# Selector scores of the second row tile computed as three products of high and low halves

## The chip, the cores and the metric

One core of one Trainium2 chip runs the kernel. The metric is the device time of one execution in microseconds. Below, TensorE is called PE in the profile, VectorE DVE, ScalarE ACT, GpSimd POOL; "L789" is line 789 of the kernel before.

## The reference, cut to what matters

The network is two layers with three kinds of attention, followed by one block of another kind (attention, convolution, feed-forward). All of it is float32, for 256 tokens of width 2048. The part that the change touches is the selector of the sparse attention ("dsa"), in each of the two layers:

```python
rel = jax.nn.relu(jnp.einsum('bqhi,bki->bqhk', qib, k_idx).astype(jnp.float32) * idx_scale)
score = jnp.einsum('bqhk,bqh->bqk', rel, wb.astype(jnp.float32))
...
_, sel = lax.top_k(score, topk)
```

There are 16 selector heads of width 64 and one selector key of width 64 per token; the 64 best keys of each query are kept. The queries are handled in two row tiles of 128 tokens. The first row tile sees 128 keys, the second 256.

## The kernel before, in words

**Weights.** The kernel streams 394 MB of weights in blocks of 128 x 1024 numbers through four buffers. For each block `g`, ACT rounds it (`round_block`, L903, `high<-raw`), DVE or POOL subtracts what was rounded off (`low_part`, L479, `low<-raw,high`; POOL takes the odd blocks 40 to 133 of a layer), and PE multiplies both parts with rounded activations and their rests (`weight_block`, L644 to L680). These products are in float32r, which PE takes in one pass; plain float32 products (attention, the selector scores) take it two instructions each.

**Order of the work.** Each layer has 162 slots `b`, one weight block each. In slot `b`, PE runs `weight_block`, then index scores, then attention work (`attention`: the values of the job from slot `b - 4`, then new scores). ACT first rounds block `b + 3` and then does `layer_side(b)`; DVE the same with `low_block(b + 3)`. So ACT and DVE are up to three blocks ahead of PE with the weights, and work on everything else in an order fixed by the program: whatever waits in `layer_side(b)` holds back the rounding of block `b + 4` and all that follows.

**The slots that matter.** Jobs of the memory attention ("mem", four heads) start in slots 64, 66, 68 and 70. A job runs: scores on PE (L727), maximum on DVE (L1319), exponentials and division on ACT (L935, L946), transposes on PE in the middle of the block of slot `+4` (L741), the copy `pt<-tb` on ACT in the same slot (`prob_copy`, L956), and right behind that block the products with the values on PE (`values`, L760 and L761), which wait for `pt_ready`. The job of slot 64 thus ends in slot 68, that of slot 68 in slot 72, that of slot 70 in slot 74. `y_high` (L966) is the job's last copy on ACT, in slot `+5`.

The selector's queries come from four weight chunks ("iq", m = 0 to 3) that end before slots 70, 74, 78 and 82. There ACT copies a part out (`cross_out`, L923), DVE adds it (`fold`, L1255) and rotates the chunk (`rope`: L1277, four times L1280 and last L1283, `work<-cb,yf`, which signals `rot_ready`). `index_scores` runs in slots 84 to 89, f = 0 to 5: f = 0 and 1 are the first row tile (eight heads, 128 keys), f = 2 to 5 the second (four heads each, 256 keys). Even heads lie on partitions 0 to 63 and write `sbank`, odd heads on 64 to 127 and write `obank`:

```python
for e, bank, full in ((0, sbank, s_full), (1, obank, o_full)):
    half = slice(64 * e, 64 * e + 64)
    for c, h in enumerate(heads[e::2]):
        q = iqT[h // 8][half, h // 2 % 4, s * P:s * P + P]
        ins = pe.matmul(bank[:, c * n:c * n + n], q, ikT[half, 0:n], start=True, stop=True)
    ins.then_inc(full, 1)
```

ACT copies both banks out with a ReLU (L1082) and DVE sums them up (L1488, L1490).

Of the kernel before, what the change touches and what calls it, by code (L numbers as in the profile page):

```python
# [36 lines left out]
ALU = mybir.AluOpType  # L37
# [154 lines left out]
SCORES2 = {58 + 8 * (h // 2) + 2 * (h % 2): ("ali", h) for h in range(H2)}  # L192

IDX_AT, TOPK_AT = 84, 90
CONV_AT, CONV_PER_2_SLOTS = 18, 8
GLU_AT = (18, 26, 42, 50)
MEAN_AT, VAR_AT, SILU_AT = 81, 83, 85
# [26 lines left out]
def build(nc, a, out):  # L224
    by, chunk_at, acc_users = plan(a)
    with ExitStack() as ctx:
        def sb(name, shape, dt=F32):
            return ctx.enter_context(nc.sbuf_tensor(name, shape, dt))
# [13 lines left out]
        yhf, ylf = yf[:, 0], yf[:, 1]  # L242
        yh, yl = yhl[:, 0], yhl[:, 1]
        x = sb("x_nat", [P, ST, D])
        work = sb("work", [P, 12528])
        cb = sb("cb", [P, 4, CW])
        sc = sb("sc", [P, 2, ST, S])
# [12 lines left out]
        def cut(t, at, *dims):  # L260

            n = int(np.prod(dims))
            v = t[:, at:at + n]
            if len(dims) == 2:
                v = v.rearrange("p (a b) -> p a b", a=dims[0])
            if len(dims) == 3:
                v = v.rearrange("p (a b c) -> p a b c", a=dims[0], b=dims[1])
            return v
# [27 lines left out]
        vm = [cut(work, 9216 + 1024 * l, ST, 512) for l in range(DEPTH)]  # L296
        ikT = cut(work, 11264, S)
        ndsa = cut(work, 11520, 512)

        q2T, k2T, v2 = cut(work, 0, H2, S), cut(work, 2048, H2, S), cut(work, 4096, ST, 1024)  # L300
        hT = cut(work, 8192, 8, PAD + S)
# [30 lines left out]
        def vec(name, n):  # L332
# [20 lines left out]
            cum_ready decay_ready rel_ready rel_used hi_ready xt_ready var_ready std_ready nmr_ready  # L353
            norm_ready aff_ready sum_ready sq_ready xres_ready rs_ready rt_ready vg2_ready qk2_ready
            sig_ready vraw_ready hT_ready conv_step low_pool yc_ready csq_ready cn_ready silu_ready ch_ready ct_ready
            relu_ready fsq_ready fin_ready out_done dve_done norm_dve rows_half""".split()
        (ident_landed, tables_landed, rows_landed, rowp_landed, rowf_landed, high_ready,
         low_ready, block_used, s_full, o_full, m_ready, e_ready, r_ready, p_ready, pt_ready, y_ready,
         yhi_ready, yt_ready, kq_ready, v_ready, g_ready, rot_ready, nar_ready, flog_in, flog_e, flog_ln,
# [1 line left out]
         hi_ready, xt_ready, var_ready, std_ready, nmr_ready, norm_ready, aff_ready, sum_ready, sq_ready,  # L361
         xres_ready, rs_ready, rt_ready, vg2_ready, qk2_ready, sig_ready, vraw_ready, hT_ready,
         conv_step, low_pool, yc_ready, csq_ready, cn_ready, silu_ready, ch_ready, ct_ready, relu_ready,
         fsq_ready, fin_ready, out_done, dve_done, norm_dve, rows_half) = (sem(n) for n in names)
        mem_landed, x_landed = ([sem(f"{n}_landed{i}") for i in range(4)] for n in ("mem", "x"))
        raw_landed = [sem(f"raw_landed{i}") for i in range(RING)]
        t_full = [sem(f"t_full{i}") for i in range(2)]
# [117 lines left out]
        def _(pe):  # L485
# [291 lines left out]
            def index_scores(l, f):  # L777
                s, n, heads = index_shape(f)
                if f == 0:

                    pe.wait_ge(ikt_ready, l + 1)
                    pe.wait_ge(rot_ready, turned(("iq", l, 3)))
                s_begin(("idx", l, f))
                o_begin(("idx", l, f))
                for e, bank, full in ((0, sbank, s_full), (1, obank, o_full)):
                    half = slice(64 * e, 64 * e + 64)
                    for c, h in enumerate(heads[e::2]):
                        q = iqT[h // 8][half, h // 2 % 4, s * P:s * P + P]
                        ins = pe.matmul(bank[:, c * n:c * n + n], q, ikT[half, 0:n], start=True, stop=True)  # L789
                    ins.then_inc(full, 1)  # L790

# [105 lines left out]
        def _(act):  # L897
# [152 lines left out]
            for l in range(DEPTH):  # L1050
                g0 = LAYER0 + LAYER_SLOTS * l

                def layer_side(b, l=l, g0=g0):
                    new = ends(g0 + b, "fq", "fk", "mq", "mg", "fg", "dg", "iq", "dq", "dk")
                    if b - 4 in SCORES:
                        prob_copy(l, *SCORES[b - 4])
                    if new:
                        cross_out(new)
                    attention(l, b, SCORES)
                    for name in (ends(g0 + b, "mv", "fv", "dv"), ends(g0 + b - 1, "fq", "fk", "mq", "mg", "fg", "dg")):  # L1060
                        if name:
                            copied_out(name)
                    if b == 10:
                        act.wait_ge(block_used, by[("nar", l)].blocks[-1] + 1)
                        act.activation(y[0:NAR, 1, :], sbank[0:NAR, 0:S], ACT.Copy).then_inc(nar_ready, 1)
                    if b == 11:

                        act.wait_ge(flog_in, l + 1)
                        act.activation(fe, fe, ACT.Exp).then_inc(flog_e, 1)
                        act.wait_ge(flog_e, l + 1)  # L1070
                        act.activation(fl, fe, ACT.Ln, bias=1.0).then_inc(flog_ln, 1)
                    if b == 150:
                        root_ahead()
                    if IDX_AT <= b < IDX_AT + 6:
                        f = b - IDX_AT
                        n = 6 * l + f
                        if n >= 2:

                            act.wait_ge(rel_used, n - 1)
                        for e, bank, full, no in ((0, sbank, s_full, s_no), (1, obank, o_full, o_no)):  # L1080
                            act.wait_ge(full, no[("idx", l, f)] + 1)
                            act.activation(rel[f % 2][e], bank[:, :], ACT.Relu, scale=IDIM ** -0.5).then_inc(rel_ready, 1)  # L1082
# [152 lines left out]
        def _(dve):  # L1235
# [168 lines left out]
            for l in range(DEPTH):  # L1404
# [16 lines left out]
                def layer_side(b, l=l, g0=g0):  # L1421
# [35 lines left out]
                        dve.wait_ge(cum_ready, l + 1)  # L1457
                    if name and name[0] in ("iq", "dq", "dk"):
                        rope(name)
                    if IDX_AT <= b < IDX_AT + 6:  # L1460
                        index_sum(l, b - IDX_AT)
                    if TOPK_AT <= b < TOPK_AT + TOPK // 8:
# [427 lines left out]
```

## Time and profile before

| | |
|---|---|
| three runs | 2184.83, 2185.27, 2188.21 us (median 2185.27) |
| the profiled execution | 2182.5 us, its span 2180.7 us |
| PE busy | 2147.4 us (98% of the span) |
| DVE busy | 1280.2 us (59%) |
| ACT busy | 1106.5 us (51%) |
| POOL busy | 405.3 us (19%) |
| mean granted clock of PE | 0.998 |

A row of a timeline gives the start, the length and the name of an instruction or of several alike that follow each other. On PE, starts are the better measure: matmuls are pipelined, so a row's length holds a tail of 0.27 to 0.4 us in which the next already runs. PE is nearly always busy, so what counts is what makes its stream longer, or stops it.

### The profile page before, as it was taken

What the parts mean: (1) busy time and instruction counts of PE and PEld (TensorE: products, weight loads), DVE (VectorE), ACT (ScalarE), POOL (GpSimd) and SP (SyncE); (2) the same over time, 40 slices, a digit from 0 to 9 for tenths busy, and PEclk for the clock granted to TensorE, in tenths of its full rate; (3) what the DMA queues carried; (4) which work ended last, traced back from release to release, by engine and by line L of the source; (5) the groups of instructions that cost most, each with busy time, mean ns of one, the idle gap of its engine ahead of it and who ended that gap; (6) DMA issues with size and microseconds to landing.
All of it is one profiled execution on the core that took longest, in us unless ns stands there. A gap on an engine that the chain in (4) does not pass through costs nothing.

```text
span 2180.7 us, 29518 instructions
## 1 busy us (share of the span) xinstructions
PE 2147.4 (98%) x11780; PEld 1863.0 (85%) x11780; DVE 1280.2 (59%) x1866; ACT 1106.5 (51%) x1537; POOL 405.3 (19%) x176
## 2 busy tenths in 40 slices
PE   8999999999999999999999999999999999999998
PEld 7888988888888898888887888788888888888886
DVE  5544438765576337856576677666555555555556
ACT  4444554554464555555455455646535534544543
POOL 0000333442000333342006886000000000000000
PEclk9999999999999999999999999999999999999999
DMA  8666555655666555665656655545566656666664
GB/s 278 196 180 184 164 149 160 177 171 174 193 187 186 162 155 155 175 173 174 189 178 183 189 179 155 198 149 181 190 194 190 191 194 191 188 193 192 190 191 140
DMA packets 324375, 394.65 MB, mean 181 GB/s; under 512 B 20320, under 2 KB 252384, under 8 KB 323472
## 3 DMA queue, kind: packets, MB, share of 16 engines
q1 hardware_dynamic: 322592, 383.20, 58.2%
q0 software_dynamic: 1648, 9.58, 1.2%
q8 instruction: 93, 1.52, 0.3%
q14 instruction: 42, 0.34, 0.0%
HBM read 390.63 MB, written 2.10 MB: 180 GB/s over the span
## 4 chain that ended last, share of the span: by engine, by line
PE 96%; DVE 2%; ACT 1%; issue 1%; DMA 0%; SPq 0%; DVEq 0%; ACTq 0%
PE acc L661 34%; PE acc L678 18%; PE acc L680 12%; PE acc L665 12%; PE acc L666 11%; PE acc L663 1%; PE acc L644 1%; PE tb L590 1%; PE obank L763 1%; PE tb L741 1%; PE sbank L731 1%; PE sbank L789 1%; ACT high L903 0%; DVE low L479 0%; ACT pt L1003 0%
## 5 line engine op out<-in xcount | busy, mean ns | idle before, releaser
L903 ACT ACTIVATE high<-raw 128x1024 fp32r<-128x1024 f32 (+1 forms) x729 | 763.1, 1050 | 791.9 <-PE acc L661 205.8
L479 DVE TENSOR_TENSOR low<-raw,high 128x1024 fp32r<-128x1024 f32 (+1 forms) x569 | 703.0, 1237 | 617.6 <-ACT high L903 614.8
L661 PE MATMUL acc<-xhl,high 128*128 128x512 f32 x3200 | 769.1, 392 | 2.9 <-ACT cb L1201 1.7
L661 PEld LDWEIGHTS acc<-xhl,high 128*128 128x128 f32 x3200 | 587.8, 189 | 117.3 <-ACT cb L1201 2.1
L479 POOL TENSOR_TENSOR low<-raw,high 128x1024 fp32r<-128x1024 f32 x160 | 397.7, 2489 | 728.7 <-ACT high L903 728.5
L678 PE MATMUL acc<-xhl,low 128*128 128x256 f32 x3200 | 435.6, 286 | 0.7 <-DVE xhl L1712 0.7
L678 PEld LDWEIGHTS acc<-xhl,low 128*128 128x128 f32 x3200 | 414.3, 191 | 16.4 <-DVE xhl L1712 1.1
L665 PE MATMUL acc<-high,yhl 128*128 128x512 f32 (+1 forms) x1044 | 383.1, 373 | 0.0
L666 PE MATMUL acc<-high,yhl 128*128 128x512 f32 (+1 forms) x1044 | 382.0, 372 | 0.0
L680 PE MATMUL acc<-low,yhl 128*128 128x512 f32 (+1 forms) x1044 | 243.7, 374 | 0.2
L665 PEld LDWEIGHTS acc<-high,yhl 128*128 128x128 f32 x1044 | 196.7, 188 | 34.3
L666 PEld LDWEIGHTS acc<-high,yhl 128*128 128x128 f32 x1044 | 196.7, 188 | 34.1
L680 PEld LDWEIGHTS acc<-low,yhl 128*128 128x128 f32 x1044 | 184.5, 189 | 34.1 <-DVE yhl L1356 1.0
L1255 DVE TENSOR_TENSOR acc<-acc,cross 128x512 f32<-128x512 f32 x104 | 72.1, 693 | 70.3 <-ACT cross L923 70.1
L1615 DVE SCALAR_TENSOR_TENSOR tb<-work,params,tb 128x256 f32<-128x256 f32 x232 | 93.5, 479 | 0.0
L935 ACT ACTIVATE sc<-sc,small 128x128 f32<-128x128 f32 x64 | 28.7, 448 | 99.2 <-DVE small L1331 99.2
L680 PE MATMUL acc<-low,xhl 128*128 128x512 f32 (+1 forms) x320 | 71.1, 355 | 0.0
L665 PE MATMUL acc<-high,xhl 128*128 128x256 f32 (+1 forms) x224 | 69.1, 331 | 0.0
L666 PE MATMUL acc<-high,xhl 128*128 128x256 f32 (+1 forms) x224 | 68.6, 329 | 0.0
L923 ACT ACTIVATE cross<-acc 128x512 f32<-128x512 f32 x104 | 60.4, 581 | 0.0
L680 PEld LDWEIGHTS acc<-low,xhl 128*128 128x128 f32 x320 | 51.8, 189 | 8.6 <-issue 1.3
L665 PEld LDWEIGHTS acc<-high,xhl 128*128 128x128 f32 x224 | 42.6, 190 | 4.8 <-issue 0.7
(214 smaller groups left out, 1355.5 us busy)
## 6 DMA issues: line engine op xcount, KB each, us to landing
raw<-in_w_in SPq DMA_DIRECT2D x336, 512.0 KB, 3.7
raw<-in_w_ff SPq DMA_DIRECT2D x256, 512.0 KB, 4.0
raw<-in_w_out SPq DMA_DIRECT2D x91, 512.0 KB, 4.4
raw<-in_w_mem_kv SPq DMA_DIRECT2D x32, 512.0 KB, 5.1
raw<-in_w_out SPq DMA_DIRECT2D x10, 256.0 KB, 2.7
x_nat<-in_mem SPq DMA_DIRECT2D x4, 512.0 KB, 7.9
x_nat<-in_x POOLq DMA_DIRECT2D x4, 512.0 KB, 6.7
yf<-in_ln_gain POOLq DMA_DIRECT2D x2, 1024.0 KB, 5.1
```

Source lines behind the costliest of these rows:

```text
L479: eng.tensor_tensor(part(low, g), part(raw, g), part(high, g).bitcast(F32), ALU.subtract).then_inc(ready, 1)
L590: ins = pe.transpose(t[:, dt * S + s * P:dt * S + s * P + P], src[:, s, first + dt * P:first + dt * P + P], ident)
L661: ins = pe.matmul(acc[:, 2 * (c.acc % 2) + s, :], wh[:, t, at], vhl, start=first, stop=last)
L665: pe.matmul(outs[s], vh[:, at], wh[:, t, :], start=first, stop=False)
L666: ins = pe.matmul(outs[s], vl[:, at], wh[:, t, :], start=False, stop=last)
L678: ins = pe.matmul(acc[:, 2 * (c.acc % 2) + s, S:2 * S], wl[:, t, at], vh, start=False, stop=last)
L680: ins = pe.matmul(outs[s], vh[:, at], wl[:, t, :], start=False, stop=last)
L903: act.activation(part(high, g), part(raw, g), ACT.Copy).then_inc(high_ready, 1)
L923: act.activation(cross, crosses(c), ACT.Copy).then_inc(cross_ready, 1)
L935: ins = act.activation(sc[:, j % 2, s, 0:n], src, ACT.Exp, bias=nmx[:, r:r + 1], accum_out=rs[:, r:r + 1])
L1255: dve.tensor_tensor(accs(c), accs(c), cross, ALU.add).then_inc(folded, 1)
L1615: ins = dve.scalar_tensor_tensor(out=cv[:, ct, :] if tap == TAPS - 1 else sums_at, in0=src, scalar=w, in1=sums_at, op0=ALU.mult, op1=ALU.add)
```

## The change

For f = 2 to 5 the float32 products are replaced by three float32r products each: rounded query by rounded key, rest of the query by rounded key, rounded query by rest of the key. The products of even and odd heads follow each other in turns. The four halves lie where the first attention's queries and keys lay (`work_r` is a float32r name for the same memory as `work`).

- ACT gets five copies in each layer: the rounded key in slot 66, the rounded queries of chunk m in slots 71, 75, 79 and 83, each at the end of the slot's side work, behind a wait for `rot_ready` of that chunk.
- DVE gets five subtractions in each layer, one slot later each, behind a wait for the ACT copy.
- PE waits for `split_ready` ahead of f = 2 to 5. f = 0 and 1 stay as they were.

```diff
 IDX_AT, TOPK_AT = 84, 90
+SPLIT_AT, IQ_SPLIT = 66, (71, 75, 79, 83)
...
+        iqH, iqL = cut(work_r, 0, IH // 2, P), cut(work_r, 1024, IH // 2, P)
+        ikH, ikL = cut(work_r, 2048, S), cut(work_r, 2304, S)
...
                 s_begin(("idx", l, f))
                 o_begin(("idx", l, f))
+                if s:
+                    pe.wait_ge(split_ready, 5 * l + f)
+                    for c in range(2):
+                        at = heads[0] // 2 + c
+                        for part_no, (q, k) in enumerate(((iqH, ikH), (iqL, ikH), (iqH, ikL))):
+                            for e, bank in enumerate((sbank, obank)):
+                                half = slice(64 * e, 64 * e + 64)
+                                ins = pe.matmul(bank[:, c * n:c * n + n], q[half, at, :], k[half, :], start=part_no == 0,
+                                                stop=part_no == 2)
+                                if c == 1 and part_no == 2:
+                                    ins.then_inc((s_full, o_full)[e], 1)
+                    return
...
+                    if b == SPLIT_AT:
+
+                        act.wait_ge(s_full, s_no[("job", job_no(l, "fox", HF - 1))] + 1)
+                        act.wait_ge(ikt_ready, l + 1)
+                        act.activation(ikH, ikT, ACT.Copy).then_inc(kh_ready, 1)
+                    if b in IQ_SPLIT:
+                        m = IQ_SPLIT.index(b)
+                        act.wait_ge(rot_ready, turned(("iq", l, m)))
+                        act.activation(iqH[:, 2 * m:2 * m + 2, :], iqT[m // 2][:, 2 * (m % 2):2 * (m % 2) + 2, P:S],
+                                       ACT.Copy).then_inc(qh_ready, 1)
...
+                    if b == SPLIT_AT + 1:
+                        dve.wait_ge(kh_ready, l + 1)
+                        dve.tensor_tensor(ikL, ikT, ikH.bitcast(F32), ALU.subtract).then_inc(split_ready, 1)
+                    if b - 1 in IQ_SPLIT:
+                        m = IQ_SPLIT.index(b - 1)
+                        dve.wait_ge(qh_ready, 4 * l + m + 1)
+                        dve.tensor_tensor(iqL[:, 2 * m:2 * m + 2, :], iqT[m // 2][:, 2 * (m % 2):2 * (m % 2) + 2, P:S],
+                                          iqH[:, 2 * m:2 * m + 2, :].bitcast(F32), ALU.subtract).then_inc(split_ready, 1)
```

ACT in slots 71 and 72 of the first layer, with the waits that stand ahead of each instruction. Before:

```order
L903 ACTIVATE high<-raw 128x1024 [waits block_used,raw_landed2]
L966 ACTIVATE yhl<-y 128x256 [waits y_ready]
L903 ACTIVATE high<-raw 128x1024 [waits block_used,raw_landed3]
L956 ACTIVATE pt<-tb 128x512 [waits o_full,t_full0]
L946 ACTIVATE sc<-sc,small 128x256 [waits r_ready]
```

With the change (lines are 19 further down):

```order
L922 ACTIVATE high<-raw 128x1024 [waits block_used,raw_landed2]
L985 ACTIVATE yhl<-y 128x256 [waits y_ready]
L1099 ACTIVATE work_r<-work 128x256 [waits rot_ready]
L922 ACTIVATE high<-raw 128x1024 [waits block_used,raw_landed3]
L975 ACTIVATE pt<-tb 128x512 [waits o_full,t_full0]
L965 ACTIVATE sc<-sc,small 128x256 [waits r_ready]
```

The copy of the rounded query and its wait now stand ahead of the rounding of block 75 and of the copy `pt<-tb` of the job from slot 68.

PE in the second row tile's scores, f = 2 of the first layer. Before (each of these float32 matmuls is two in the trace):

```order
L789 MATMUL sbank<-work 128x256 [waits rel_ready]
L789 MATMUL sbank<-work 128x256
L789 MATMUL obank<-work 128x256 x2
```

With the change:

```order
L799 MATMUL sbank<-work_r 128x256 [waits split_ready,rel_ready]
L799 MATMUL obank<-work_r 128x256
L799 MATMUL sbank<-work_r 128x256
L799 MATMUL obank<-work_r 128x256
L799 MATMUL sbank<-work_r 128x256
L799 MATMUL obank<-work_r 128x256
L799 MATMUL sbank<-work_r 128x256
L799 MATMUL obank<-work_r 128x256
L799 MATMUL sbank<-work_r 128x256
L799 MATMUL obank<-work_r 128x256
L799 MATMUL sbank<-work_r 128x256
L799 MATMUL obank<-work_r 128x256
```

Four products in float32 have become twelve in float32r, in turns between the two banks.

## Rows read from the trace of the kernel before

**Rows 1.** The page: busy times; a costly group: count, busy us, mean ns, idle before.

```profile
PE 2147.4 (98%) x11780; PEld 1863.0 (85%) x11780; DVE 1280.2 (59%) x1866; ACT 1106.5 (51%) x1537; POOL 405.3 (19%) x176
...
L678 PE MATMUL acc<-xhl,low 128*128 128x256 f32 x3200 | 435.6, 286 | 0.7 <-DVE xhl L1712 0.7
```

**Rows 2.** PE's timeline at f = 3, first layer: start us, length us, engine, line, names.

```profile
379.63 0.39 PE L666 MATMUL acc<-high,xhl 128*128 128x512 f32 x1
379.94 0.48 PE L789 MATMUL sbank<-work 64*128 64x256 f32 x1
379.96 0.48 PE L789 MATMUL obank<-work 64*128 64x256 f32 x1
380.26 0.38 PE L789 MATMUL sbank<-work 64*128 64x256 f32 x1
...
380.70 0.38 PE L789 MATMUL sbank<-work 64*128 64x256 f32 x1
...
381.35 0.40 PE L666 MATMUL acc<-high,xhl 128*128 128x512 f32 x1
```

**Rows 3.** The same view at f = 0, end of it: weight loads, then matmuls.

```profile
367.61 0.63 PEld L789 LDWEIGHTS obank<-work 64*128 64x128 f32 x5
...
367.72 0.72 PE L789 MATMUL obank<-work 64*128 64x128 f32 x5
```

**Rows 4.** PE's timeline, a run of float32r matmuls of 256 columns on the whole array.

```profile
599.84 4.00 PE L796 MATMUL sbank<-xhl 128*128 128x256 f32 x32
```

**Rows 5.** ACT's timeline, slots 67 to 76 of the first layer.

```profile
312.19 1.05 ACT L903 ACTIVATE high<-raw 128x1024 fp32r<-128x1024 f32 x1
...
314.60 0.60 ACT L956 ACTIVATE pt<-tb 128x512 f32<-128x512 f32 x1
...
328.65 0.41 ACT L966 ACTIVATE yhl<-y 128x256 fp32r<-128x256 f32 x1
328.95 1.05 ACT L903 ACTIVATE high<-raw 128x1024 fp32r<-128x1024 f32 x1
330.11 0.60 ACT L956 ACTIVATE pt<-tb 128x512 f32<-128x512 f32 x1
...
337.38 0.57 ACT L956 ACTIVATE pt<-tb 128x512 f32<-128x512 f32 x1
...
342.04 1.06 ACT L903 ACTIVATE high<-raw 128x1024 fp32r<-128x1024 f32 x1 [1.97 <-PE acc L661]
```

**Rows 6.** PE's timeline: the values of the jobs from slots 64, 68 and 70.

```profile
315.35 0.62 PE L760 MATMUL obank<-pt,work 128*128 128x256 f32 x2
...
330.86 0.62 PE L760 MATMUL obank<-pt,work 128*128 128x256 f32 x2
...
336.72 1.19 PE L678 MATMUL acc<-xhl,low 128*128 128x256 f32 x8
338.06 0.67 PE L760 MATMUL obank<-pt,work 128*128 128x256 f32 x2
```

**Rows 7.** DVE's timeline: the last step of rope for m = 0 and 1.

```profile
330.19 2.81 DVE L1283 TENSOR_TENSOR work<-cb,yf 128x512 f32<-128x512 f32 x1
...
343.86 2.27 DVE L1283 TENSOR_TENSOR work<-cb,yf 128x512 f32<-128x512 f32 x1
```

**Rows 8.** All instructions of line 1283 in that form: shortest, median, longest in ns.

```profile
L1283 DVE TENSOR_TENSOR work<-cb,yf x16: 692/693/2816, 330.2 to 1004.7; 128x512 f32<-128x512 f32 x16
```

**Rows 9.** POOL's timeline in slot 72.

```profile
330.08 2.37 POOL L479 TENSOR_TENSOR low<-raw,high 128x1024 fp32r<-128x1024 f32 x1 [5.20 <-ACT high L903]
```

**Rows 10.** The second layer, slot 72: ACT's timeline, then PE's.

```profile
832.63 0.60 ACT L956 ACTIVATE pt<-tb 128x512 f32<-128x512 f32 x1
...
833.38 0.62 PE L760 MATMUL obank<-pt,work 128*128 128x256 f32 x2
```

**Rows 11.** The last block: PE's timeline; then the stretch behind it (third number from the end: PE's clock).

```profile
1380.94 0.67 PE L763 MATMUL obank<-pt,work 128*128 128x256 f32 x2 [3.37 <-issue]
...
1381.00:1383.00 2.00, 2.00 (x10) 1.73 (x11) 1.93 (x3) 1.97 (x5) 0.00 (x0) 1.00 0.56 178
```

More of the change, by code:

```diff
@@ L244, in build @@
         x = sb("x_nat", [P, ST, D])
+        with nc.sbuf_tensor("work_r", [P, 12528], F32R) as work_r:
+            pass
         work = sb("work", [P, 12528])
@@ L355, in build @@
             sig_ready vraw_ready hT_ready conv_step low_pool yc_ready csq_ready cn_ready silu_ready ch_ready ct_ready
-            relu_ready fsq_ready fin_ready out_done dve_done norm_dve rows_half""".split()
+            relu_ready fsq_ready fin_ready out_done dve_done norm_dve rows_half kh_ready qh_ready split_ready""".split()
         (ident_landed, tables_landed, rows_landed, rowp_landed, rowf_landed, high_ready,
@@ L363, in build @@
          conv_step, low_pool, yc_ready, csq_ready, cn_ready, silu_ready, ch_ready, ct_ready, relu_ready,
-         fsq_ready, fin_ready, out_done, dve_done, norm_dve, rows_half) = (sem(n) for n in names)
+         fsq_ready, fin_ready, out_done, dve_done, norm_dve, rows_half, kh_ready, qh_ready, split_ready) = (sem(n) for n in names)
         mem_landed, x_landed = ([sem(f"{n}_landed{i}") for i in range(4)] for n in ("mem", "x"))
@@ L787, in index_scores @@
                     for c, h in enumerate(heads[e::2]):
-                        q = iqT[h // 8][half, h // 2 % 4, s * P:s * P + P]
+                        q = iqT[h // 8][half, h // 2 % 4, 0:P]
                         ins = pe.matmul(bank[:, c * n:c * n + n], q, ikT[half, 0:n], start=True, stop=True)
```

## The prediction

> **What bounds the kernel now.** I read the page first. PE is busy for 98% of the span [rows 1], so nothing that another engine gains can shorten the run. The change can act in two ways: by the length of PE's own stream, and by new stops in it. I then read the stretch of the scores on PE's timeline. The reader is to see that even and odd heads already run side by side, though the program issues them one after the other: `obank` starts 0.02 us behind `sbank` [rows 2]. So the change cannot win by pairing the halves. Last I read ACT's timeline ahead of the scores beside that of PE, since ACT works in program order, and looked for what stands behind the new waits. What matters there is `pt<-tb`. PE starts the products with the values 0.11 us after the copy has ended where it waited for it (337.38 + 0.57 = 337.95, start at 338.06) [rows 5, 6].
>
> **The part on PE: the scores.** At f = 3 the last ordinary matmul starts at 379.63; ordinary ones of 512 columns follow each other every 0.23 us, so the next would have been due at 379.86. The second one behind the scores starts at 381.35, which puts the stream back in step at 381.12. The pass costs 1.26 us [rows 2]. It holds four pairs of float32 instructions, (380.70 - 380.26) / 2 = 0.22 us apart, hence 4 x 0.22 = 0.88, and 0.38 us for going to half-height tiles and back, which stays.
>
> With the change there are six pairs. A float32r matmul of 256 columns on the whole array comes every (4.00 - 0.28) / 31 = 0.12 us [rows 4]. I take that for a pair, since pairs are seen to start together [rows 2]: 6 x 0.12 + 0.38 = 1.10 us, a gain of 0.16 us. There are eight such passes (f = 2 to 5, two layers): **-1.3 us**. No row shows float32r on half the rows, so the bounds are: 0.11 us a pair, the pace of the shortest matmuls on one half [rows 3], which gives 1.04 and -1.8 us in all; and the halves in turns, 12 x 0.12 + 0.38 = 1.82, which gives +4.5 us in all.
>
> **The weight loads.** In one half, five loads start (0.63 - 0.19) / 4 = 0.11 us apart (0.19 us is the length of one) and the matmuls (0.72 - 0.27) / 4 = 0.11 us apart [rows 3]. A load thus runs while the matmul before it, in the same half, still streams. The Trainium skill (TensorE: Matmul & The Clock Gate, Part 3, The mechanism) says that a weight load overlaps running matmuls only when its row group is another one, which speaks against this change, as each half gets six loads for four. By that rule the sum below would be 5.3 us higher (second rival); rows 3 contradict it, with pairs in one half at 0.11 us.
>
> **The part on ACT: the key, slot 66.** The new copy is like `y_high`, 0.41 us long, and puts off what follows by 0.30 us (328.65 to 328.95), as copies overlap a little [rows 5]. It stands ahead of the rounding at 312.19, and from there ACT has no gap up to the copy `pt<-tb` at 314.60. That copy ended at 315.20 and will end at 315.50; the values start 0.11 us later at 315.61 instead of 315.35 [rows 5, 6]: **+0.3 us** of PE per layer.
>
> **The part on ACT: the queries of m = 0, slot 71.** This is the main term. ACT reaches the new wait when `y_high` is done, at about 329.0. The chunk's rope then still has its last step before it: it begins at 330.19 [rows 5, 7]. Behind the wait stand the rounding of block 75 (now at 328.95) and `pt<-tb` (now at 330.11). How long the last step takes is the question. It took 2.81 us, but that form has a median of 0.693 us [rows 7, 8]. It was stretched while POOL subtracted block 75 from 330.08 to 332.45 [rows 9], and POOL could only do so because ACT had rounded block 75. With ACT held, POOL has nothing, and the step ends at 330.19 + 0.69 = 330.88. The Trainium skill (SBUF — State Buffer, SBUF: two separate sides) calls the pair of ports that DVE and GpSimd share an exclusive lock, held for a whole instruction, also against DVE operations with two SBUF inputs. By it the step should be short when POOL is idle; the trace agrees, as the 2.81 us step ended 0.55 us after POOL's.
>
> So: copy of the queries 330.92, rounding of block 75 from 331.22, `pt<-tb` 0.95 us later (1.05 less the overlap) from 332.17 to 332.77, values at 332.88. Before they started at 330.86 [rows 6]: **+2.0 us** of PE per layer. The second layer stands the same, with `pt<-tb` at 832.63 and values at 833.38 [rows 10], 0.75 us apart as before (330.11 and 330.86).
>
> **What is given back.** The values of the next job started at 338.06 while PE's matmuls ahead of it, from 336.72, were out of the way at 336.72 + 1.19 - 0.29 + 0.13 = 337.75 [rows 1, 6]. That stop of 0.3 us came from ACT being late, since it stood behind the long rope step. With rope over two us earlier and PE two us later, it goes: **-0.3 us** per layer.
>
> **Edits costed at nothing.** m = 1 holds ACT in slot 75 from about 340.1 until rope ends. That end moves from 346.13 to 343.86 + 0.69 = 344.55, again as POOL is idle [rows 7]. Block 79 is then rounded from about 344.9 instead of 342.04 and POOL has its rest at about 348.4. PE needs it three blocks after 342.04; a block is 8 x 0.23 + 8 x 0.12 = 2.8 us, so at 350.4. The cover is 2 us; without it the same stop as in slot 72 would come. No `pt<-tb` stands behind this wait, nor behind those of m = 2 and 3. Behind the last, in slot 83, stand a rounding and the copies of the scores' first banks, which come later than rope ends. DVE's five subtractions of some 0.4 us find DVE 59% busy [rows 1], waiting for PE's values or ACT's roundings around them; if one meets POOL it is late by up to 2.4 us, inside the three blocks that DVE is ahead. PE's new waits ahead of f = 2 to 5 are for queries split in slots 72 to 84, and it gets to them in slots 86 to 89. SP's loads for blocks 79 and 83 are issued 2 to 3 us later, as they wait for POOL's rests; their cover is again the three blocks by which ACT is ahead.
>
> **The clock.** A stop of 3.37 us for the same reason (`pt<-tb` late) stands in the last block, and the stretch behind it shows a granted clock of 1.00, the 2.4 GHz level [rows 11]. A stop of 2.0 us should cost nothing more.
>
> **Sum.** 2 x (0.3 + 2.0 - 0.3) - 1.3 = **+2.7 us** on the profiled execution's 2182.5: 2185.2 us. That execution lies 2.8 us below the median of the three runs, so for the runs I carry +2.7 over to the median: **2188.0 us**. A measurement of this kernel can tell about 0.2%, or 4.4 us, from no change; +2.7 is less.
>
> **Rivals.**
> - *Rope stays long, slower (chance 0.13).* If the last step of rope takes its 2.81 us with POOL idle too, the values of slot 72 wait 2.1 us longer in each layer: +2.7 + 4.2 = +6.9, 2192.2 us. It decides from a step of about 1.6 us on. For it: two of the long steps are just these chunks'. Against it: the median of 0.693 us, and POOL's end 0.55 us before the step's [rows 8, 9].
> - *The halves lose their overlap, slower (0.15).* If a half must finish a product before it takes its next weights, each product takes 0.11 + 0.12 = 0.23 us, a pass 6 x 0.23 + 0.38 = 1.76, and eight passes +4.0 instead of -1.3: +8.0 in all, 2193.3 us. Halves strictly in turns give +8.5. For it: twelve loads where there were eight, in turns. Against it: rows 2 and 3. The Trainium skill's rule named above would be this case.
> - *No stop at all (0.12).* If PE were held at slot 72 by nothing new, because rope and the rounding came earlier than I place them, only the gain in the scores is left: -1.3, 2184.0 us. For it: ACT has gaps on both sides of slot 72. Against it: between wait and values only 0.11 us of slack is seen.
> - *The change does nothing for the scores (inside my forecast).* At 0.147 us a pair a pass costs the same as before and the sum is +4.0.
>
> **How the numbers follow.** The forecast has 0.55, with a range of its own from +0.8 to +4.8; 0.05 is left for longer stops, such as POOL and DVE meeting on a path that matters. The range reaches from the third rival with the scatter of the runs, 2183.5, to the second with the same, 2194. Slower by over 0.2%: the first two rivals, the 0.05, and the upper edge of the forecast, 0.35. Faster by over 0.2% has no mechanism but scatter, 0.03. Within 0.2%: 0.62.
>
> **What would show it.** In the new profile: a pass of the scores of about 1.1 us, six pairs 0.12 us apart; ACT's new copy in slot 71 behind a wait of about 2 us for DVE's rope; L1283's steps of iq all at 0.69 us; PE idle for about 2 us ahead of the values of slot 72, once in each layer, and not ahead of those of slot 74; PE's clock at 1.00 after it. I am wrong if pairs are 0.2 us apart, if PE stops in slots 75 to 89, or if it does not stop in slot 72.

## Result, and the profile after

The changed kernel took **2191.56 us** (median of 12 runs, 2187.25 to 2193.95), beside 2184.94 us for the kernel before (12 runs, 2183.10 to 2188.21). The ratio is **1.0027, 95% interval 1.0018 to 1.0035**: 5.9 us slower, with an interval of 3.9 to 7.6. The forecast was 2.7 us slower and 2188.0 us. The time lies inside the range given, but above the forecast's own +0.8 to +4.8, and past the 0.2% that I had taken as the border of "no change".

The profiled execution took 2191.48 us (span 2189.4) beside 2182.5 (span 2180.7). That is 9.0 us, more than the 5.9 us of the medians; what the rest is, the part on the last block shows. The page hardly shows the difference, since PE is busy at 98% in both; the line answers to [rows 1]:

```profile
PE 2151.1 (98%) x11812; PEld 1867.5 (85%) x11812; DVE 1278.7 (58%) x1876; ACT 1109.6 (51%) x1547; POOL 406.1 (19%) x176
```

The list of what PE waited for does. Here `L767` is the line that was 760, the values `pt` times V, and it had no entry before; `L770` is the old 763, unchanged:

```profile
PE obank L767 <- issue: 3.7, 2, 1.8
PE obank L770 <- issue: 3.4, 1, 3.4
```

Two stops of 1.84 us. PE's timeline around the first, to be laid beside [rows 6]:

```profile
314.58 0.67 PE L767 MATMUL obank<-pt,work 128*128 128x256 f32 x2
...
329.11 1.19 PE L685 MATMUL acc<-xhl,low 128*128 128x256 f32 x8
332.14 0.67 PE L767 MATMUL obank<-pt,work 128*128 128x256 f32 x2 [1.84 <-issue]
...
332.89 2.00 PE L685 MATMUL acc<-xhl,low 128*128 128x256 f32 x8
334.68 4.73 PE L668 MATMUL acc<-xhl,high 128*128 128x512 f32 x16
...
339.61 1.19 PE L685 MATMUL acc<-xhl,low 128*128 128x256 f32 x8
340.64 0.62 PE L767 MATMUL obank<-pt,work 128*128 128x256 f32 x2
```

How to read it: subtract the start of the same instruction before. The values were at 315.35, 330.86 and 338.06; they are at 314.58, 332.14 and 340.64. The lag goes from -0.77 to +1.28 to +2.58 us. The first step, 2.05 us, is the stop. The second, 1.30 us, has no stop in it. It is 1.61 us lost less 0.31 us given back at the values of slot 74. The loss shows in the matmuls: eight of `L685` take 2.00 us where they take 1.30 us in the same place before. The table by stretches says why (the length stands ahead of the comma, PE's busy time behind it, and PE's clock is the third number from the end):

```profile
330.00:332.10 2.10, 0.30 (x3) 0.09 (x1) 1.78 (x4) 1.91 (x4) 0.47 (x1) 1.00 0.00 0
332.10:334.00 1.90, 1.86 (x9) 1.79 (x10) 0.72 (x2) 1.90 (x4) 1.90 (x1) 0.79 0.74 189
334.00:336.00 2.00, 2.00 (x9) 1.71 (x8) 1.80 (x3) 0.15 (x1) 0.04 (x1) 0.50 0.59 139
336.00:338.00 2.00, 2.00 (x9) 1.65 (x8) 0.00 (x0) 0.33 (x1) 0.00 (x0) 0.85 0.94 262
```

Behind the stop the granted clock is 0.50, the 1.2 GHz level, and PE is busy all the same. The second layer is a copy of the first, `L685` at 2.27 us:

```profile
837.66 0.67 PE L767 MATMUL obank<-pt,work 128*128 128x256 f32 x2 [1.84 <-issue]
...
838.47 2.27 PE L685 MATMUL acc<-xhl,low 128*128 128x256 f32 x8
```

The cause of the stop itself, on ACT and DVE in slots 71 and 72, answers to [rows 5, 7]:

```profile
330.19 0.42 ACT L1099 ACTIVATE work_r<-work 128x256 fp32r<-128x256 f32 x1 [1.86 <-DVE work L1312]
330.51 1.04 ACT L922 ACTIVATE high<-raw 128x1024 fp32r<-128x1024 f32 x1
331.46 0.58 ACT L975 ACTIVATE pt<-tb 128x512 f32<-128x512 f32 x1
```

```profile
329.46 0.69 DVE L1312 TENSOR_TENSOR work<-cb,yf 128x512 f32<-128x512 f32 x1
```

ACT is held 1.86 us for rope, then rounds block 75, and only then copies `pt<-tb`, which ends at 332.04; the values start at 332.14. Rope's last step took 0.69 us, where it had taken 2.81. All sixteen in that form now lie between 692 and 695 ns, for a largest of 2816 before [rows 8]. POOL is idle meanwhile, as its next row shows:

```profile
331.63 2.41 POOL L486 TENSOR_TENSOR low<-raw,high 128x1024 fp32r<-128x1024 f32 x1 [7.48 <-ACT high L922]
```

The Trainium skill (SBUF — State Buffer, SBUF: two separate sides) has DVE and GpSimd exclude each other on a shared pair of ports. By that page the step should be short with POOL idle, and the trace agrees.

The scores of the second row tile at f = 3, first layer, beside [rows 2]:

```profile
382.04 0.39 PE L673 MATMUL acc<-high,xhl 128*128 128x512 f32 x1
382.36 0.38 PE L799 MATMUL sbank<-work_r 64*128 64x256 f32 x1
382.36 0.38 PE L799 MATMUL obank<-work_r 64*128 64x256 f32 x1
382.58 0.28 PE L799 MATMUL sbank<-work_r 64*128 64x256 f32 x1
...
382.70 0.28 PE L799 MATMUL sbank<-work_r 64*128 64x256 f32 x1
...
383.05 0.27 PE L799 MATMUL sbank<-work_r 64*128 64x256 f32 x1
...
383.60 0.40 PE L673 MATMUL acc<-high,xhl 128*128 128x512 f32 x1
```

Both halves run together, in pairs (383.05 - 382.58) / 4 = 0.12 us apart, and the pass costs (383.60 - 0.23) - (382.04 + 0.23) = 1.10 us, where it cost 1.26. The weight loads of one half follow each other as closely, each while a matmul of its own half streams (PE's loads at f = 2, then its matmuls):

```profile
378.70 0.18 PEld L799 LDWEIGHTS sbank<-work_r 64*128 64x128 f32 x1
...
378.81 0.19 PEld L799 LDWEIGHTS sbank<-work_r 64*128 64x128 f32 x1
```

```profile
378.69 0.28 PE L799 MATMUL sbank<-work_r 64*128 64x256 f32 x1
...
378.81 0.28 PE L799 MATMUL sbank<-work_r 64*128 64x256 f32 x1
```

### The profile page after: what moved, and what is told of

Same layout as the page of the kernel before. It is cut to its first block, busy times and chain, and to the rows that moved or that the text cites. A ratio compares the mean times of both kernels' runs of the same rounds, so it can differ in the third digit from the quotient of the medians.

```text
span 2189.4 us, 29604 instructions
## 1 busy us (share of the span) xinstructions
PE 2151.1 (98%) x11812; PEld 1867.5 (85%) x11812; DVE 1278.7 (58%) x1876; ACT 1109.6 (51%) x1547; POOL 406.1 (19%) x176
## 3 DMA queue, kind: packets, MB, share of 16 engines
q8 instruction: 94, 1.54, 0.3%
## 4 chain that ended last, share of the span: by engine, by line
PE 96%; DVE 1%; ACT 1%; issue 1%; DMA 1%; SPq 0%; DVEq 0%; ACTq 0%
PE acc L668 35%; PE acc L685 18%; PE acc L687 12%; PE acc L672 11%; PE acc L673 11%; PE acc L670 1%; PE acc L651 1%; PE tb L597 1%; PE obank L770 1%; PE tb L748 1%; PE sbank L738 1%; ACT high L922 0%; ACT pt L1022 0%; PE sbank L737 0%; PE obank L771 0%
## 5 line engine op out<-in xcount | busy, mean ns | idle before, releaser
L685 PE MATMUL acc<-xhl,low 128*128 128x256 f32 x3200 | 437.6, 287 | 0.7 <-DVE xhl L1749 0.7
L685 PEld LDWEIGHTS acc<-xhl,low 128*128 128x128 f32 x3200 | 416.3, 192 | 16.6 <-DVE xhl L1749 1.1
```

Source lines behind the costliest of these rows:

```text
L685: ins = pe.matmul(acc[:, 2 * (c.acc % 2) + s, S:2 * S], wl[:, t, at], vh, start=False, stop=last)
```

## The experiments

Profiled executions start up to 1.4 us apart, and runs of one kernel scatter by some 3 to 4 us to either side, so I use one measure beside the ratio: **the stretch** from the start of the first `sbank<-work` pair of 128 columns past 279 us to that of the first past 950 us. It takes in the scores of both layers and the slots ahead of them, all that the change touches. In the profile of before the two rows are (the second behind the last scores):

```profile
282.73 0.39 PE L730 MATMUL sbank<-work 128*128 128x128 f32 x2
...
955.71 0.39 PE L730 MATMUL sbank<-work 128*128 128x128 f32 x2
```

In the profile after they stand at line 737:

```profile
281.75 0.39 PE L737 MATMUL sbank<-work 128*128 128x128 f32 x2
...
960.73 0.39 PE L737 MATMUL sbank<-work 128*128 128x128 f32 x2
```

So 672.98 before and 678.98 after, +6.00. A second number, **values to values**, is the time from the values of slot 72 to those of slot 74 (332.14 and 340.64 above: 8.50); a slow clock shows in it, a stop ahead of slot 72 does not.

| kernel | stretch, against before | stop ahead of slot 72, per layer | values to values, first layer | ratio of the runs (95%), runs |
|---|---|---|---|---|
| after | +6.00 | 1.84 idle | 8.50 | 1.0027 (1.0018 to 1.0035), 12 |
| after_again | +6.09 | 1.84 idle | 8.54 | 1.0028 (1.0016 to 1.0040), 6 |
| e1_m0_later | +3.19 | none | 7.53, with a stop of 0.47 | 1.0026 (1.0016 to 1.0037), 9 |
| e2_all_later | -0.46 | none | 7.52, with a stop of 0.47 | 1.0011 (1.0002 to 1.0021), 11 |
| e3_wait_only | +2.76 | 1.54 idle | 6.94 | 1.0015 (1.0006 to 1.0024), 11 |
| e4_scores_f32 | +3.88 | 1.84 idle | 6.93 | 1.0026 (1.0017 to 1.0035), 11 |
| e5_stop_filled | +2.90 | filled | 6.94 | 1.0017 (1.0008 to 1.0026), 11 |
| e6_halves_apart | +1.55 | none | 7.20 | 1.0031 (1.0019 to 1.0042), 6 |
| e7_split_late | -0.99 | none | 7.21 | 1.0008 (0.9997 to 1.0018), 11 |
| e7b_split_late_again | -0.99 | none | 7.21 | 1.0001 (0.9991 to 1.0011), 12 |
| e8_split_late_f32 | +0.05 | none | 7.21 | 1.0009 (1.0000 to 1.0017), 11 |
| e10_split_late_shifted | +0.04 | none | 7.23 | 1.0000 (0.9992 to 1.0009), 12 |
| c0_before_again | +0.05 | none | 7.20 | 0.9992 (0.9983 to 1.0000), 11 |

A ratio of 1.001 is 2.2 us. Two kernels that are the same give the same stretch within 0.1 us, while their ratios lie up to 0.0008 from each other or from 1. The 7.20 us of before and of c0, and the 7.20 to 7.23 of e6, e7, e8 and e10, hold the 0.3 us stop of slot 74 [rows 6]; 6.94 is the distance without it.

My theory was the prediction's: ACT held in slot 71 makes `pt<-tb` late, and a later slot for the copy frees it. The rival: ACT is then held elsewhere, and the stop is handed on.

**The wait alone.** The kernel before, with nothing but the new wait on ACT; no copy, no subtraction, no new scores.

```diff
+                    if b == 71:
+                        act.wait_ge(rot_ready, turned(("iq", l, 0)))
```

> The kernel before plus one bare wait: ACT waits for the rotation of m = 0 at the end of slot 71, and does nothing there. Nothing else of the change is in it. Theory 1: PE stops ahead of the values of slot 72 for 0.3 us less than in the changed kernel (no copy behind the wait), 1.7 us, rope's last step is 0.69 us long, 0.3 us comes back in slot 74, and behind each stop PE's clock falls to 1.2 GHz for some us (1.7 us each): 2184.9 + 2 x (1.7 - 0.3 + 1.7) = 2191.1 us, or 2187.7 if a stop of 1.7 us leaves the clock up. Theory 2: within 1 us of before.

```profile
332.78 0.67 PE L760 MATMUL obank<-pt,work 128*128 128x256 f32 x2 [1.54 <-issue]
...
334.67 3.83 PE L661 MATMUL acc<-xhl,high 128*128 128x512 f32 x16
...
339.72 0.62 PE L760 MATMUL obank<-pt,work 128*128 128x256 f32 x2
```

The wait alone makes the stop; the copy itself adds the 0.30 us to 1.84. Per layer: +1.69 of stop, -0.31 given back, 2.76 in all. So the stop comes from what the wait holds back on ACT, not from any work that was added. The clock stayed up behind it here (`L661` x16 at 3.83 us), which the expectation held possible; the median of the runs, 2189.44 us, lies between its two figures, 2191.1 and 2187.7.

**The scores undone, the copies kept.** As after, but the second tile's scores are the float32 products again; the split halves are made and not used.

```diff
                 if s:
                     pe.wait_ge(split_ready, 5 * l + f)
-                    for c in range(2):
...
-                    return
...
-                        q = iqT[h // 8][half, h // 2 % 4, 0:P]
+                        q = iqT[h // 8][half, h // 2 % 4, s * P:s * P + P]
```

> The changed kernel with its copies, subtractions and waits, but the second row tile's scores in plain float32 as before. Theory 1: slower than the changed kernel by what the new products gain, 1.3 us: 2192.9 us, ratio to before 1.0036. Theory 2 (the new products save nothing, or lose): the same time as the changed kernel or less.

The stops are the same 1.84 us in both layers, but the clock did not fall behind either of them in this profiled execution: values to values 6.93 and 6.94 us, where after has 8.50 and 8.53. The stretch is +3.88. Against e5's +2.90, which has the same slots and a full clock too, the scores are worth 0.98 us; e7 against e8 gives 1.04. The forecast was 1.3. The ratios (1.0026 beside after's 1.0027) read as the expectation's second theory, that the new products save nothing. They can't show that, since after's profile has the two spells of slow clock and e4's has not, and a microsecond is less than their scatter.

**The stop filled.** As after, with 16 matmuls whose result nobody reads in the place of the stop. They begin once the last exponent of the job has left `sbank`.

```diff
+                if table is SCORES and b == 72:
+                    pe.wait_ge(e_ready, job_no(l, "mem", 3) + 1)
+                    for _ in range(16):
+                        pe.matmul(sbank[:, 0:S], xh[:, 0, 0:P], xh[:, 0, :], start=True, stop=True)
```

> The changed kernel with 16 matmuls more in slot 72 of each layer, ahead of the products with the values: float32r, 256 columns, on data that is at hand, into a bank that nobody reads. Theory 1 (PE stops for 2 us, and because it stood still its clock falls behind the stop): the values still start when pt<-tb is done, 2.0 us late, but PE is busy until then, and the clock stays at 2.4 GHz in both layers. The profile of the changed kernel lost 1.6 us a layer there, so up to 3.2 us less than the changed kernel's 2191.6: 2188.4 us. Theory 2 (the low clock there is chance and costs little on average): the same as the changed kernel within 1 us.

```profile
331.24 2.08 PE L778 MATMUL sbank<-xhl 128*128 128x256 f32 x16
333.25 0.67 PE L767 MATMUL obank<-pt,work 128*128 128x256 f32 x2
...
335.14 3.83 PE L668 MATMUL acc<-xhl,high 128*128 128x512 f32 x16
```

```profile
333.00:335.00 2.00, 2.00 (x14) 1.79 (x13) 0.61 (x2) 2.00 (x5) 2.00 (x1) 1.00 0.62 167
```

The values are as late as in after, 3.04 us behind the `L685` group of 330.21 (after: 332.14 - 329.11 = 3.03), and nothing was saved in waiting. Yet the stretch is 3.1 us shorter than after's, because the clock stays at 1.00. This separates the two parts of the loss: 2.9 us of lateness and other terms, 3.1 us of clock. The runs agree in direction (1.0017 beside 1.0027, median 2188.52 us for the 2188.4 expected), but the intervals overlap.

**The copies moved.** Same work, other slots. The row of numbers is (key, m = 0 to 3).

```diff
-SPLIT_AT, IQ_SPLIT = 66, (71, 75, 79, 83)
+SPLIT_AT, IQ_SPLIT = 66, (72, 75, 79, 83)
```

> The changed kernel with one number changed: the copy of the rounded queries of m = 0 stands in slot 72, behind the copy pt<-tb, not in slot 71. Theory 1 (the cost is the stop ahead of the values of slot 72, and the lower clock behind it): that stop goes in both layers, so does the half-speed stretch; left are the scores' gain of 1.3 us and 0.3 us a layer from the key's copy in slot 66. Expected 2184.9 - 1.3 + 0.6 = 2184.2 us, ratio to before 0.9997 +- 0.0008. Theory 2 (the waits of m = 1 to 3 or the added work on ACT and DVE cost it): at most the 2 x 2.0 us seen as idle go, the ratio stays at 1.001 or above.

This missed. The stop of slot 72 is gone, as theory had it, but the stretch is still +3.19. 0.3 us comes back at slot 74, and 1.5 us per layer in slots 75 to 84. ACT and POOL of that stretch (the time in brackets is idle time before, and what ended it):

```profile
345.96 0.42 ACT L1099 ACTIVATE work_r<-work 128x256 fp32r<-128x256 f32 x1 [4.52 <-DVE work L1312]
...
347.40 4.96 POOL L486 TENSOR_TENSOR low<-raw,high 128x1024 fp32r<-128x1024 f32 x2 [7.03 <-ACT high L922]
```

DVE beside them, and two of the places where PE then stops:

```profile
347.44 2.66 DVE L1495 TENSOR_TENSOR work_r<-work,work_r 128x256 fp32r<-128x256 f32 x1
350.02 3.43 DVE L486 TENSOR_TENSOR low<-raw,high 128x1024 fp32r<-128x1024 f32 x1
```

```profile
362.43 1.20 PE L687 MATMUL acc<-low,xhl 128*128 128x512 f32 x4 [0.73 <-POOL low L486]
...
368.62 0.79 PE L808 MATMUL sbank<-work 64*128 64x128 f32 x5 [0.45 <-issue]
```

The wait of m = 1 holds ACT for 4.52 us, as long as in the kernel after (4.51), but PE is now 2.2 us further on. ACT then hands over three roundings in a row, where after has two and then waits for PE. POOL and DVE meet on them: a subtraction that takes DVE 0.42 us takes 2.66 (in after too), and the next, 1.21 us in after, takes 3.43. Rope of the next chunk is late for that, and ACT's next wait grows from 3.50 us in after to 6.67. PE's first stop, from 361.7 us on, comes behind that wait of m = 2; behind m = 1 there is none. That the bunching is what makes this wait long is read from the rows; no run takes it out alone. The prediction had costed m = 1 to 3 at nothing on the cover of three blocks, with the sum worked out for m = 1 only. In the kernel after it held for all, but with PE itself 2 us late; with PE on time it did not hold for m = 2. The rival is right in part: the stop is handed on, at 1.5 us for 2.

```diff
+SPLIT_AT, IQ_SPLIT = 63, (72, 76, 80, 84)
```

> All four copies of the queries one slot later (72, 76, 80, 84), the key's copy in slot 63, where ACT idles. Theory 1: no stop is left at all and PE gains what the scores give, 1.3 us: 2183.6 us, ratio 0.9994 +- 0.0008, 0.6 us below the run with only m = 0 moved. Theory 2: if m = 1 to 3 or the key cost more than I think, this one is faster than the run with only m = 0 moved by clearly over 1 us.

The stretch is -0.46, which is 3.65 less than e1's, so the expectation's second theory holds: the other copies had cost more than I thought. The stops of slots 75 to 84 are gone; 0.3 us per layer is left at slot 74, where the copy of slot 72 now stands in ACT's chain ahead of `pt<-tb`.

```diff
+SPLIT_AT, IQ_SPLIT = 63, (74, 78, 82, 84)
```

> The key's copy in slot 63, the queries' copies in slots 74, 78, 82 and 84, where ACT does not wait for them and none stands ahead of a pt<-tb that PE waits for. Theory 1: no new stop in either layer, scores 0.53 us shorter per layer: by the trace 1.1 us less than before outside the low-clock stretches, 2184.2 us, ratio 0.9995. Theory 3 (the extra copies and subtractions cost something of their own, or the program is disturbed elsewhere): clearly slower than before, like the run with all copies one slot later, 1.0010 or above.

```profile
331.00 0.62 PE L767 MATMUL obank<-pt,work 128*128 128x256 f32 x2
...
338.21 0.67 PE L767 MATMUL obank<-pt,work 128*128 128x256 f32 x2
```

```profile
338.49 0.41 ACT L1099 ACTIVATE work_r<-work 128x256 fp32r<-128x256 f32 x1
```

No new stop is left (the old one of 0.3 us at slot 74 is there, as before): the rotated chunk is ready when ACT gets to its copy. The stretch is -0.99, which is the gain of the scores and no more, twice over (e7 and its repeat). The runs do not show it: 1.0008, and 1.0001 when repeated. With float32 scores in the same slots:

> As the run with the copies in slots 63, 74, 78, 82 and 84, but the scores in plain float32 as before: all the added work of ACT and DVE, nothing of the new products. Theory 1: exactly before, 2185.3 us, ratio 1.0000 +- 0.0008, and 1.1 us above its twin. Theory 3: 1.0010 or above, here too.

The stretch is +0.05, so the five copies and five subtractions cost nothing there, and the scores are worth the 1.04 us between e7 and e8. By the ratios (1.0008 and 1.0001 for e7, 1.0009 for e8) one microsecond can't be resolved: e8 lies between the 1.0000 of its first theory and the 1.0010 of its third.

**The halves apart.** e7 with another order of the same twelve products: the six of the even heads first, then the six of the odd.

```diff
-                    for c in range(2):
...
+                    for e, bank in enumerate((sbank, obank)):
...
+                        for c in range(2):
...
+                            for part_no, (q, k) in enumerate(((iqH, ikH), (iqL, ikH), (iqH, ikL))):
...
```

> As the run with the copies in slots 63, 74, 78, 82 and 84, but the twelve products of a pass in another order: first the six of the even heads, then the six of the odd ones, not in turns. Theory 1 (a half runs ahead of the other only by what PE's queue lets it): as at f = 0 before, the odd half starts when three or so products of the even half are left, so a pass takes about 9 x 0.12 + 0.38 = 1.5 us instead of 1.1: +0.35 x 8 = 2.8 us against its twin. Theory 2 (order does not matter, each half has a queue of its own): the same as its twin.

```profile
379.27 0.39 PE L673 MATMUL acc<-high,xhl 128*128 128x512 f32 x1
379.59 0.62 PE L799 MATMUL sbank<-work_r 64*128 64x256 f32 x3
379.93 0.38 PE L799 MATMUL obank<-work_r 64*128 64x256 f32 x1
...
380.39 0.52 PE L799 MATMUL obank<-work_r 64*128 64x256 f32 x3
...
381.17 0.39 PE L673 MATMUL acc<-high,xhl 128*128 128x512 f32 x1
```

The odd half starts three products late, and a pass takes (381.17 - 0.23) - (379.27 + 0.23) = 1.44 us for 1.10. Over eight passes that makes 2.7 us; the stretches differ by 1.55 + 0.99 = 2.54, as expected (+2.8). So the turns in which the change issues its products earn their keep. In the kernel before, four products with two instructions each were side by side even in sequence [rows 2]; with six per half that no longer holds.

**What is the last part's doing?** Past 955 us nothing was changed, but there the ratios and the stretches come apart. Three runs look at that: the kernel before itself, after itself, and e7 with nine matmuls added in slot 100 of the second layer, which make it late by the 1 us that it had gained.

> The kernel before, unchanged, in the place of a changed one. It shows what two sets of runs of one and the same kernel differ by. Theory R (where PE's clock falls in the last block is chance, drawn anew in each execution): ratio 1.0000 +- 0.0010, with medians up to 2 us apart. Theory P (it hangs on when PE comes to the last block's stops): ratio 1.0000 +- 0.0005, at most one execution in five above 2188 us.

> The changed kernel again: 2191 us +- 1 by either theory, as its stops ahead of the values of slot 72 and the low clock behind them stay.

> The kernel with the copies in slots 63, 74, 78, 82 and 84 again. By its trace it is 1.0 us shorter than before up to the last block, and yet over half its executions were above 2188 us. Theory R: that was chance; median 2184 to 2186. Theory P: it comes again; median about 2188, and half the executions above it.

> As the run with the copies in slots 63, 74, 78, 82 and 84, with nine idle matmuls (1.1 us) in slot 100 of the second layer, which puts PE's arrival in the last block back to where it is before the change. Theory R: 1.1 us above its twin. Theory P: the slow executions become as rare as before, so it is below its twin by about 1 us in the median although it does more.

Before against itself: 0.9992 (0.9983 to 1.0000), so a ratio is good to about 0.001, or 2 us. After repeats: stops of 1.84 us, the slow clock behind both, +6.09 in the stretch, 1.0028. e10 is at 1.0000 although its stretch is 1.03 us longer than e7's. What decides there is the clock, and it differs from execution to execution. PE stops for 3.37 us ahead of `L763` in every kernel. In the profile of before the clock was 1.00 behind it [rows 11]. This is the same kernel in its second profile (PE's timeline, then the stretches behind):

```profile
1380.90 1.19 PE L763 MATMUL obank<-pt,work 128*128 128x256 f32 x2 [3.38 <-issue]
```

```profile
1381.00:1383.00 2.00, 2.00 (x6) 1.72 (x7) 1.88 (x3) 1.97 (x5) 0.00 (x0) 0.50 0.51 169
1383.00:1385.00 2.00, 2.00 (x8) 1.53 (x8) 0.89 (x1) 2.00 (x5) 0.00 (x0) 0.74 0.75 232
```

The pair of matmuls takes 1.19 us where it had taken 0.67. In 14 profiled executions it is 0.67 in three (before, after, e8) and 1.19 in eleven. The row on which I had rested the clock was the rarer case of its own stop.

There are three such places in the last block, behind stops that end near 1155, 1381 and 1460 us in before. The table gives PE's mean granted clock in 20 us around each, and the time from the pair near 955 us to the end of the span:

| profiles | 1150:1170 | 1378:1398 | 1458:1478 | last part, us |
|---|---|---|---|---|
| before, e8 | 0.91 | 1.00 | 1.00 | 1225.0, 1226.6 |
| after | 0.91 | 1.00 | 0.91 | 1228.7 |
| c0, e1, e4, after_again | 0.83 | 0.91 | 1.00 | 1227.3, 1229.3, 1228.4, 1229.9 |
| e3, e6 | 0.91 | 0.83 | 0.91 | 1229.1, 1230.9 |
| e2 | 0.83 | 0.91 | 0.91 | 1232.3 |
| e10 | 0.83 | 0.83 | 0.91 | 1231.8 |
| e5, e7, e7b | 0.91 | 0.83 | 0.83 | 1232.0, 1232.8, 1232.6 |

By and large, the lower the clock in the three together, the longer the last part: by up to 8 us, with nothing changed there. What is left, up to 3 us between profiles with the same three clocks, the table does not explain. The microsecond that e7 gained drowns in this. It also splits the two profiled spans: of the 8.7 us between before and after, 6.0 are the stretch, 3.7 lie behind it, and after is 1.0 us earlier at its start.

The other executions have a mean clock on record too, and their time goes with it. Of the 89 executions of the kernel before that ran beside the experiments, the 14 at 0.998 took 2182.9 us on average, the 55 at 0.996 2185.3 and the 15 at 0.994 2188.6. That makes a count possible. Above 2188 us lie 11 of the 23 executions of e7 and its repeat, but only 13 of 92 of the kernels that reach the last block as late as before does (9 of 58 of before itself beside e7 and its repeat, 0 of 11 of c0, 2 of 11 of e8, 2 of 12 of e10). So the slow executions are more frequent in e7 than chance would have it, and the nine added matmuls go with few of them again, which speaks for the moment of PE's arrival (theory P). Its other half, a median 1 us below the twin, is met against e7 (2186.0 beside 2188.47) and not against the repeat (2185.55). How the arrival would act on the clock is not shown.

## Why the prediction was right, and where it was not

| step | forecast | profiled execution |
|---|---|---|
| key in slot 66, per layer | +0.3 | +0.28, +0.27 |
| stop at slot 72, per layer | +2.0 | +1.99, +2.00 |
| given back at slot 74 | -0.3 | -0.31, -0.31 |
| scores, both layers | -1.3 | -1.0 (e5 to e4; e8 to e7) |
| m = 1 to 3, key and query subtractions | 0 | 0, with PE late |
| clock behind the stops, per layer | 0 | +1.61, +1.63 |
| sum | +2.7 | +6.0 (the stretch); without the clock, +2.8 (its 6.0 less 3.2) |

(The values of the middle column are steps of the lag at the same instruction: -0.99 us ahead of slot 66, -0.71 behind it, +1.28 at the values of slot 72, +2.89 at 336 us, +2.58 at the values of slot 74; the second layer likewise from 2.01.)

**What held.** The main term and its whole chain: ACT held in slot 71, rope's step at 0.69 us because POOL has no block yet, rounding, `pt<-tb`, values 0.1 us behind. The stop came out at 1.99 us of PE time for 2.0, and e3 shows that the wait alone makes it. The pass of the scores is 1.10 us, as worked out; the eight of them brought 1.0 instead of 1.3, that is 0.13 us each on average, where f = 3 shows 0.16. The first rival (rope stays long) is out by the 0.69 us, the third (no stop) by the timeline. The third had been summed at -1.3 us, without the key's +0.3 us a layer, which does not hang on slot 72; with it, it would have been -0.7. The second (the halves lose their overlap) is out by pairs 0.12 us apart and 1.10 us a pass. With it goes the rule that the Trainium skill gives (TensorE: Matmul & The Clock Gate, Part 3, The mechanism), that a load overlaps running matmuls only in another row group: here, loads and matmuls of one half both come every 0.11 to 0.12 us. (The same section of the Trainium skill also lets a load go ahead into a background weight buffer, which is compatible with these rows; they can't tell.) e6 is the nearest that a run came to it: 2.5 us more than e7, from the order of issue.

**The step that failed** is "The clock": "A stop of 2.0 us should cost nothing more." It rested on one stop of 3.37 us with a clock of 1.00 behind it [rows 11]. That row was true of one execution; in eleven of the fourteen profiled ones the clock fell to 0.50 at that very stop, in the same kernel's second profile too. Behind the 1.84 us stops the clock fell in four cases of four in the two profiles of after, and in none of two in e4's. When it falls, it costs 1.6 us; e5, which keeps the lateness and fills the stop, has no fall and gives +2.90. So a term of 3.2 us had been put at nothing, and the forecast's own range, up to +4.8, missed the measured +5.9; only the rivals' ends of the wider range held it. The term should have been "between 0 and 1.6 us per layer", which puts the forecast at +2.7 to +5.9. That range alone would have moved much of the chance from "within 0.2%" to slower. The term of the scores was too large as well, 1.0 for 1.3 us, since it took the pass at f = 3 for all eight.

**What held by luck.** m = 1 to 3 cost nothing only behind a late PE; e1 shows 1.5 us per layer as soon as PE is on time. And the time came out inside the range for another reason than the range was built on: its upper end stood for halves that lose their overlap, which they do not.

**What stays open.** What lets the clock fall behind one stop of 1.84 us and not behind another, and how often it does so in the runs that were not profiled. Their mean clocks give a hint: after's two executions at 0.998 took 2187.3 and 2188.3 us, near the 2188.0 of the forecast, and at that mean before's profile has one short fall only while PE works, near 1154 us, which all fourteen have. So those two had most likely none behind the stops of slot 72. Against before at the same clock they are still 4.9 us slower, and the four at 0.994 (2193.2) 4.6 us, more than the 2.8 us that the stretch shows without its falls; the remaining 2 us are not explained. After's ratio of 1.0027 is what both falls would give, but e4 and e1, whose stretches are 2 to 3 us shorter, come out at 1.0026. Their intervals reach down to 1.0017 and 1.0016, so part of that is scatter, and part is the last block. No version beat the kernel before in the runs; e7 is the best of them in the stretch, by 1.0 us of 2185 (e2 by 0.5), and the best that can be said of it is "the same".

## What to carry to other kernels

A wait added to an in-order engine is priced by what stands behind it, not by the work it guards: here a 0.41 us copy cost PE 2 us a layer because a copy that PE needed stood two instructions further on. When PE is at 98%, a stop of some 2 us can have a second price, a spell at the lower clock that cost 1.6 us here and may or may not fall due in a given execution. Put it in the range in full, and don't rule it out from one row. A gain of 1 us of 2185 can drown in what the clock does hundreds of microseconds later, so compare the clocks of the two profiles there before trusting a ratio. An edit that was costed at nothing because of a lead of some blocks should be costed again for the case that the main loss is repaired, since the repair takes the lead away.

## What the runs showed of the hardware that I had not expected

- The clock fell to 0.50 behind all four stops of 1.84 us in after's two profiles and behind neither in e4's; behind one stop of 3.37 us it fell in eleven executions and stayed at 1.00 in three. The length of the stop alone did not decide it.
- With PE fed continuously and useless work in the gap, the clock held, and the stretch was 3.1 us shorter though not one instruction was ready sooner.
- A half of the array with six products ahead of it in the queue is not reached by the other half's until three are left: 1.44 us for 1.10, the same twelve products in another order.
- When POOL and DVE meet, both of DVE's kinds of subtraction lose over 2 us: 0.42 to 2.66 and 1.22 to 3.43 us.
- In a part that no version changed, 14 profiled executions differ by up to 8 us (1225.0 to 1232.8), largely in step with the granted clock behind three stops.
